# Two-part fp32 matmuls of a streaming trunk: the order of long and short matmuls inside a chunk of weights

## The chip, the core and the metric

The kernel runs on one core of one Trainium2 chip. The metric is device time in microseconds, from the start to the end of an execution; the profile is of one such execution.

## What is computed

A trunk of two layers on 256 tokens of width 2048, in float32. Each layer is a token mixer and a squared-ReLU MLP, both behind an RMSNorm and added to the stream:

```
for layer in range(2):
    hn = rms_norm(h, mix_norm[layer])
    mix = swa_sink_attention(hn, ...) if layer == 0 else rglru_block(hn, ...)
    h = h + mix
    h = h + jnp.square(relu(rms_norm(h, mlp_norm[layer]) @ w_up[layer])) @ w_down[layer]
return rms_norm(h, final_norm)
```

The widths are 2048 to 2560 (query, key, value), 2048 to 2048 (attention's output), 2048 to 8192 to 2048 (each MLP), 2048 to 4096 (into the recurrent block) and 2048 to 2048 (out of it). Nearly all work is in these products.

## The kernel before

Everything is kept transposed: 128 channels on the partitions, the 256 tokens along a row. A product `w.T @ x` takes a 128 x 128 piece of the weights as the stationary operand and the tokens as the moving one.

**Two parts.** Weights and activations are each split into a high part, rounded to the matmul's fp32r type, and a low part, the rest. Of the four partial products three are made. A *long* matmul (L1307) takes the high weights and streams 512 columns, the 256 tokens' high parts and then their low parts, into the two halves of a PSUM bank. A *short* one (L1310) takes the low weights and streams the 256 high parts into the second half of the same bank, where they are added.

**Tiling.** Weights come in chunks of 512 input rows by 256 output columns (512 KB), already laid out so in memory. Four chunks (`CHUNKS`) cover the 2048 input rows and make a pair: two blocks (`b`) of 128 output columns, in two PSUM banks. Two pairs are a quad (512 output columns), and `ps` has a bank for each of its four blocks. In a chunk there are four row blocks (`CH_KT`, index `k`) and two column blocks `b`, so 8 long and 8 short matmuls. `products` issues them: for each `k` long `b`=0, long `b`=1, short `b`=0, short `b`=1. The text calls these four a group. There are 85 quads, 680 chunks.

**Who does what.** SyncE loads chunks into 8 slots (`w_raw`), each as soon as VectorE has made the low half of the slot's chunk before. ScalarE copies a chunk to `w_hi` (L370, `next_hi`), VectorE subtracts for `w_lo` (L812, `next_lo`). `w_hi` and `w_lo` have four slots, one for each chunk of a pair, so a slot is refilled when TensorE has done the same chunk of the pair before: the last short matmul of a chunk raises `wts_used`. Before a chunk TensorE waits for `lo_ready`, for the operand (`xn_ready` or `mid_ready`) and, before the first chunk of a pair, for `psum_free`. At a pair's end ScalarE copies the second halves of the banks out (L383), VectorE adds the first halves (L826), and the pair's own step follows: rope and softmax, the residual sum and the next norm's operand, or the squared ReLU.

**The order of the work** is written out by hand. Each engine runs attention's 5 quads, the output's 4, an MLP of 32, the recurrent mixer's 8 and 4, and the second MLP of 32. An MLP has four turns of four quads up and four quads down. The MLP's norm needs the sum over all channels of the squares: `stats(norm)`, two small fp32 matmuls (L1334 and L1335) that TensorE makes behind the first pair of the MLP; ScalarE then takes the root (L412) and VectorE its inverse (L836). Attention puts scores, transposes and outputs between chunks (`between` of `pair`), the recurrent mixer its gates: `gates` makes 24 matmuls of the short one's shape through `three` (L1327 to L1329), each three adding to the same 256 columns. `late_quad` is the first quad of each output product, whose last chunk has weight tiles of its own, `gate_hi` and `gate_lo`. The execution ends with sums (L1496) and 16 and more 128 x 128 transposes (L1489).

Of the kernel before, what the change touches and what calls it, by code (L numbers as in the profile page):

```python
# [27 lines left out]
PART = 128  # L28
TOK = 256
D = 2048  # L30
KT = D // PART
# [11 lines left out]
CH_KT = 4  # L43
PAIR_N = 256
CHUNKS = KT // CH_KT
WARM_UP = 22
SLOTS = 2 * CHUNKS

# [8 lines left out]
QB_IN = QB_MLP0 + Q_MLP  # L57
# [60 lines left out]
def build(nc, x_l, vec_d, const_d, w_qkv, w_o, w_in, ga_w, gx_w, w_out, w_up, w_down, out_l):  # L118
# [12 lines left out]
    with ctx:  # L131
# [1164 lines left out]
        def _(pe):  # L1296
            def products(q, half_i, s, operand, ready_sem, ready, late=False):

                pe.wait_ge(lo_ready, (q * 2 + half_i) * CHUNKS + s + 1)
                if s == 0 and not (isinstance(q, int) and q == 0):  # L1300
                    pe.wait_ge(psum_free, q * 2 + half_i - 1)
                pe.wait_ge(ready_sem, ready + 2 * s + 2)
                hi, lo = late_w if late else (w_hi[:, s], w_lo[:, s])
                for k in range(CH_KT):
                    kt = s * CH_KT + k
                    for b in range(2):
                        nc.tensor.matmul(ps[:, 2 * half_i + b, :], hi[:, k, b * PART:(b + 1) * PART],  # L1307
                                         operand[:, :, kt, :], start=kt == 0, stop=False)
                    for b in range(2):
                        last = nc.tensor.matmul(ps[:, 2 * half_i + b, TOK:2 * TOK], lo[:, k, b * PART:(b + 1) * PART],  # L1310
                                                operand[:, 0, kt, :], start=False, stop=kt == KT - 1)
                last.then_inc(wts_used, 1)

            def pair(q, half_i, operand, ready_sem, ready, between=None):

                for s in range(CHUNKS):
                    products(q, half_i, s, operand, ready_sem, ready)
                    if between and s in between:
                        between[s]()

            def quad(q, operand, ready_sem, ready, between=None, between_b=None):
                pair(q, 0, operand, ready_sem, ready, between)
                pair(q, 1, operand, ready_sem, ready, between_b)

# [85 lines left out]
            def attention_pair(q, half_i, j, g, g_before):  # L1410

                between = {3: lambda: scores_and_output(j, g, g_before)}
                if g_before is not None:
                    between[2] = lambda: transpose_probs(j - 1)
                pair(q, half_i, *qkv, between)

# [28 lines left out]
            def mlp(base, norm, mid_base):  # L1445
                operand = (xn, xn_ready, 8 * norm)
                quad(base, *operand, {3: lambda: stats(norm)})
                with pe.Fori(1, 4) as i:
                    quad(i + base, *operand)
                with pe.Fori(0, 4) as i:  # L1450
                    quad(i + (base + 4), mid, mid_ready, mid_base)
                with pe.Fori(1, GROUPS) as g:
                    with pe.Fori(0, 4) as i:
                        quad(g * 8 + i + base, *operand)
                    with pe.Fori(0, 4) as i:
                        quad(g * 8 + i + (base + 4), mid, mid_ready, g * PAIRS + mid_base)

# [123 lines left out]
```

## Time and profile before

| | us |
|---|---|
| median of 3 runs | 1996.04 (1995.44 to 1996.25) |
| the profiled execution | 1995.82 |
| its span, first to last instruction | 1993.7 |
| TensorE busy | 1982.3 (99%) |
| weight loads busy | 1736.9 (87%) |
| VectorE busy | 1368.5 (69%) |
| ScalarE busy | 1062.1 (53%) |

The span is the time between the first and the last instruction in the profile, on which all times in its rows are counted. Of an engine's rows the duration runs from the start of an instruction to its end; TensorE's matmuls overlap, so the time that one costs is read from start to start. In a timeline row "x2" are two instructions of one kind in a row, with the time from the first one's start to the last one's end.

### The profile page before, as it was taken

How to read it: one execution, taken by the hardware profiler on the slowest of the kernel's cores; microseconds unless marked ns; L12 is line 12 of the kernel's file. 1: busy time of each engine (PE TensorE's matmuls, PEld its weight loads, DVE VectorE, ACT ScalarE, POOL GpSimd, SP SyncE). 2: the span in 40 equal slices, each digit the busy share in tenths (PEclk: the TensorE clock that was granted, in tenths of full speed). 3: DMA queues.
4: the chain of work that ended last, by engine and by line, in shares of the span. 5: the costliest groups of instructions: out<-in, count | busy, mean ns of one | idle time of the engine just before them, and what ended most of it. 6: DMA issues, size and time to landing. Idle time of an engine off the chain costs nothing.

```text
span 1993.7 us, 34015 instructions
## 1 busy us (share of the span) xinstructions
PE 1982.3 (99%) x11542; PEld 1736.9 (87%) x11542; DVE 1368.5 (69%) x1575; ACT 1062.1 (53%) x1446; POOL 7.4 (0%) x11
## 2 busy tenths in 40 slices
PE   9999999999999999999999999999999999999998
PEld 8898888888888888888888888888888888888887
DVE  8998676556656665666789997766566556656664
ACT  6666554444444444445588885544444444444453
POOL 1000000000000000000000000000000000000000
PEclk9999999999999999999999999999999999999999
DMA  7434555555555555555555545565556555555652
GB/s 287 158 127 158 181 189 191 188 191 188 189 190 180 197 186 191 177 175 199 190 190 189 189 169 192 188 197 184 193 184 187 192 182 197 189 189 178 195 175 95
DMA packets 104187, 368.17 MB, mean 185 GB/s; under 512 B 11472, under 2 KB 15696, under 8 KB 104016
## 3 DMA queue, kind: packets, MB, share of 16 engines
q1 hardware_dynamic: 103856, 365.53, 55.4%
q0 software_dynamic: 288, 2.10, 0.3%
q8 instruction: 24, 0.39, 0.1%
q14 instruction: 19, 0.16, 0.0%
HBM read 365.48 MB, written 2.10 MB: 184 GB/s over the span
## 4 chain that ended last, share of the span: by engine, by line
PE 94%; DVE 3%; ACT 2%; issue 1%; DVEq 0%; ACTq 0%; POOL 0%; POOLq 0%
PE ps L1307 61%; PE ps L1310 30%; DVE w_lo L812 1%; ACT h L467 1%; PE aux L1327 1%; PE aux L1328 1%; PE aux L1329 1%; PE aux L1399 0%; ACT w_hi L370 0%; DVE h L923 0%; DVE h L934 0%; PE aux L1382 0%; DVE u L826 0%; DVE pt L939 0%; DVE u L899 0%
## 5 line engine op out<-in xcount | busy, mean ns | idle before, releaser
L812 DVE TENSOR_TENSOR w_lo<-w_raw,w_hi 128x1024 fp32r<-128x1024 f32 x678 | 815.8, 1222 | 336.2 <-ACT w_hi L370 335.1
L370 ACT ACTIVATE w_hi<-w_raw 128x1024 fp32r<-128x1024 f32 x678 | 701.4, 1054 | 448.3 <-PE ps L1310 445.5
L1307 PE MATMUL ps<-xn,w_hi 128*128 128x512 f32 x2880 | 906.4, 396 | 0.2 <-DVE w_lo L812 0.2
L1307 PE MATMUL ps<-mid,w_hi 128*128 128x512 f32 x2544 | 799.4, 396 | 1.1 <-DVE w_lo L812 0.6
L1310 PEld LDWEIGHTS ps<-xn,w_lo 128*128 128x128 f32 x2880 | 541.0, 188 | 127.9
L1310 PEld LDWEIGHTS ps<-mid,w_lo 128*128 128x128 f32 x2544 | 477.9, 188 | 113.0
L1310 PE MATMUL ps<-xn,w_lo 128*128 128x256 f32 x2880 | 566.1, 278 | 0.0
L1310 PE MATMUL ps<-mid,w_lo 128*128 128x256 f32 x2544 | 499.9, 278 | 0.0
L1307 PEld LDWEIGHTS ps<-xn,w_hi 128*128 128x128 f32 x2880 | 438.9, 189 | 1.2 <-issue 0.5
L1307 PEld LDWEIGHTS ps<-mid,w_hi 128*128 128x128 f32 x2544 | 387.3, 189 | 1.8 <-DVE w_lo L812 1.0
L826 DVE TENSOR_TENSOR u<-ps,half 128x512 f32<-128x512 f32 x169 | 116.6, 690 | 155.3 <-ACT half L383 136.0
L383 ACT ACTIVATE half<-ps 128x512 f32<-128x512 f32 x153 | 91.6, 599 | 228.7 <-PE ps L1310 228.7
L594 ACT ACTIVATE mid<-u 128x512 f32 (+1 forms) x64 | 40.6, 634 | 105.4 <-DVE u L1054 105.4
L1060 DVE TENSOR_TENSOR mid<-v,mid 128x512 f32 (+1 forms) x64 | 44.3, 693 | 23.0 <-ACT mid L594 22.8
L852 DVE TENSOR_TENSOR h<-h,u 128x512 f32 (+1 forms) x70 | 48.5, 693 | 11.6 <-DVE u L826 11.5
L842 DVE SCALAR_TENSOR_TENSOR xn<-h,vec,xn (+1 forms) x48 | 21.1, 482 | 40.3 <-ACT xn L405 40.3
L1057 DVE TENSOR_TENSOR v<-u 128x512 f32<-128x512 f32 x64 | 44.3, 692 | 2.2
L1054 DVE SCALAR_TENSOR_TENSOR u<-u,rstd 128x512 f32<-128x512 f32 x64 | 44.3, 692 | 2.2
L403 ACT ACTIVATE sq<-h 128x512 f32 (+1 forms) x24 | 15.2, 632 | 41.5 <-DVE h L852 40.0
L831 DVE TENSOR_TENSOR acc<-acc,sq 128x512 f32<-128x512 f32 x31 | 21.3, 687 | 5.8 <-ACT sq L772 5.8
L1181 DVE SCALAR_TENSOR_TENSOR xc<-xb,vec,xc 128x256 f32<-128x256 f32 x48 | 21.1, 481 | 4.3 <-ACT xc L686 2.6
L467 ACT ACTIVATE h<-aux,h 128x128 f32<-128x128 f32 x64 | 22.4, 374 | 0.0
(168 smaller groups left out, 762.0 us busy)
## 6 DMA issues: line engine op xcount, KB each, us to landing
w_raw<-mlp_w_up_dram SPq DMA_DIRECT2D x256, 512.0 KB, 4.2
w_raw<-mlp_w_down_dram SPq DMA_DIRECT2D x256, 512.0 KB, 4.2
w_raw<-b_w_in_dram SPq DMA_DIRECT2D x64, 512.0 KB, 4.9
w_raw<-a_w_qkv_dram SPq DMA_DIRECT2D x40, 512.0 KB, 4.8
w_raw<-a_w_o_dram SPq DMA_DIRECT2D x32, 512.0 KB, 4.5
w_raw<-b_w_out_dram SPq DMA_DIRECT2D x32, 512.0 KB, 4.4
h<-x_l_dram SPq DMA_DIRECT2D x4, 512.0 KB, 8.1
gate_raw<-b_gate_a_w_dram SPq DMA_DIRECT2D x8, 256.0 KB, 2.8
```

Source lines behind the costliest of these rows:

```text
L370: nc.scalar.activation(w_hi[:, s, :, :], w_raw[:, slot, :, :], ACT.Copy).then_inc(hi_ready, 1)
L383: nc.scalar.activation(half[:, :, :], src, ACT.Copy).then_inc(half_copied, 1)
L467: last = nc.scalar.activation(out[:, m * PART:(m + 1) * PART], xs[:, b, (m % 4) * PART:(m % 4 + 1) * PART], ACT.Exp, bias=s_neg[:, m:m + 1 ...
L594: nc.scalar.activation(mid[:, 0, bass.ds(j * 2, 2), :], u[:, :, :], ACT.Square).then_inc(mid_hi, 1)
L812: nc.vector.tensor_tensor(w_lo[:, s, :, :], w_raw[:, slot, :, :], w_hi[:, s, :, :].bitcast(F32), ALU.subtract).then_inc(lo_ready, 1)
L826: nc.vector.tensor_tensor(u[:, :, :], ps[:, 2 * half_i:2 * half_i + 2, 0:TOK], half[:, :, :], ALU.add).then_inc(psum_free, 1)
L852: add = nc.vector.tensor_tensor(h_pair(j), h_pair(j), u[:, :, :], ALU.add)
L1054: nc.vector.scalar_tensor_tensor(u[:, :, :], in0=u[:, :, :], scalar=0.0, in1=bc2(rstd[:, :]), op0=ALU.max, op1=ALU.mult).then_inc(relu_rea ...
L1057: nc.vector.tensor_tensor(v[:, :, :], u[:, :, :], u[:, :, :], ALU.mult).then_inc(squared, 1)
L1060: nc.vector.tensor_tensor(mid[:, 1, bass.ds(j * 2, 2), :], v[:, :, :], mid[:, 0, bass.ds(j * 2, 2), :].bitcast(F32), ALU.subtract).then_in ...
L1307: nc.tensor.matmul(ps[:, 2 * half_i + b, :], hi[:, k, b * PART:(b + 1) * PART], operand[:, :, kt, :], start=kt == 0, stop=False)
L1310: last = nc.tensor.matmul(ps[:, 2 * half_i + b, TOK:2 * TOK], lo[:, k, b * PART:(b + 1) * PART], operand[:, 0, kt, :], start=False, stop=k ...
```

## The change

The matmuls of a chunk are now issued by two small functions, `long` and `short`, and `products` has two orders. The old one stays for the first and late quads, for attention's output and the mixers' first pairs. The new one (`in_turn`) takes for each `b` the four `k`, and for each a long and then its short matmul. It is used for the first three chunks of six attention pairs, for the recurrent mixer's quads from the second on, and for all quads of both MLPs but the first one; there the first pair keeps the old order. The second pair of that quad, behind `stats`, is issued by a new function `apart`: 24 long matmuls of three chunks, then their 24 short ones, then the fourth chunk in turn. Each chunk's waits stand ahead of its long matmuls, and `wts_used` rises behind its short ones.

```diff
+RUN = 3
...
-            def products(q, half_i, s, operand, ready_sem, ready, late=False):
+            def chunk_ready(q, half_i, s, ready_sem, ready):
                 pe.wait_ge(lo_ready, (q * 2 + half_i) * CHUNKS + s + 1)
                 if s == 0 and not (isinstance(q, int) and q == 0):
                     pe.wait_ge(psum_free, q * 2 + half_i - 1)
                 pe.wait_ge(ready_sem, ready + 2 * s + 2)
+            def long(half_i, hi, s, k, b, operand):
+                kt = s * CH_KT + k
+                nc.tensor.matmul(ps[:, 2 * half_i + b, :], hi[:, k, b * PART:(b + 1) * PART],
+                                 operand[:, :, kt, :], start=kt == 0, stop=False)
+            def short(half_i, lo, s, k, b, operand):
+                kt = s * CH_KT + k
+                return nc.tensor.matmul(ps[:, 2 * half_i + b, TOK:2 * TOK], lo[:, k, b * PART:(b + 1) * PART],
+                                        operand[:, 0, kt, :], start=False, stop=kt == KT - 1)
+            def products(q, half_i, s, operand, ready_sem, ready, late=False, in_turn=False):
+                chunk_ready(q, half_i, s, ready_sem, ready)
                 hi, lo = late_w if late else (w_hi[:, s], w_lo[:, s])
...
+                if in_turn:
                     for b in range(2):
+                        for k in range(CH_KT):
+                            long(half_i, hi, s, k, b, operand)
+                            last = short(half_i, lo, s, k, b, operand)
+                else:
+                    for k in range(CH_KT):
+                        long(half_i, hi, s, k, 0, operand)
+                        long(half_i, hi, s, k, 1, operand)
+                        short(half_i, lo, s, k, 0, operand)
+                        last = short(half_i, lo, s, k, 1, operand)
                 last.then_inc(wts_used, 1)
...
+            def apart(q, half_i, operand, ready_sem, ready):
+                for s in range(RUN):
+                    chunk_ready(q, half_i, s, ready_sem, ready)
+                    for k in range(CH_KT):
+                        for b in range(2):
+                            long(half_i, w_hi[:, s], s, k, b, operand)
+                for s in range(RUN):
+                    for k in range(CH_KT):
+                        for b in range(2):
+                            last = short(half_i, w_lo[:, s], s, k, b, operand)
+                    last.then_inc(wts_used, 1)
+                for s in range(RUN, CHUNKS):
+                    products(q, half_i, s, operand, ready_sem, ready, in_turn=True)
...
-                pair(q, half_i, *qkv, between)
+                pair(q, half_i, *qkv, between, (0, 1, 2) if g_before is not None else ())
...
+            whole = tuple(range(CHUNKS))
...
-                quad(base, *operand, {3: lambda: stats(norm)})
+                pair(base, 0, *operand, {3: lambda: stats(norm)})
+                apart(base, 1, *operand)
                 with pe.Fori(1, 4) as i:
-                    quad(i + base, *operand)
+                    quad(i + base, *operand, None, whole)
                 with pe.Fori(0, 4) as i:
-                    quad(i + (base + 4), mid, mid_ready, mid_base)
+                    quad(i + (base + 4), mid, mid_ready, mid_base, None, whole)
...
-                quad(n + QB_IN, *lru_in, {0: lambda: gates(n - 1)})
+                quad(n + QB_IN, *lru_in, {0: lambda: gates(n - 1)}, whole)
```

How the instructions move on TensorE is seen at two places. The first is a chunk in the loop over an MLP's second to fourth quads, before:

```order
L1299 REGISTER_ALU
L1307 MATMUL ps<-xn,w_hi 128x512 [waits xn_ready,lo_ready]
L1307 MATMUL ps<-xn,w_hi 128x512
L1310 MATMUL ps<-xn,w_lo 128x256 x2
L1307 MATMUL ps<-xn,w_hi 128x512 x2
L1310 MATMUL ps<-xn,w_lo 128x256 x2
```

and now, its first half (the long matmul is L1308 and the short one L1314 there):

```order
L1300 REGISTER_ALU
L1308 MATMUL ps<-xn,w_hi 128x512 [waits xn_ready,lo_ready]
L1314 MATMUL ps<-xn,w_lo 128x256
L1308 MATMUL ps<-xn,w_hi 128x512
L1314 MATMUL ps<-xn,w_lo 128x256
L1308 MATMUL ps<-xn,w_hi 128x512
L1314 MATMUL ps<-xn,w_lo 128x256
```

The two long ones of a group stood side by side, and the two short ones; now every short one stands between two long ones. The waits are the same, ahead of the chunk's first matmul.

The second place is TensorE behind the sum of squares of the first MLP (`aux<-acc,ones` are the two matmuls of `stats`), before:

```order
L1334 MATMUL aux<-acc,ones 128x256 [waits acc_ready]
L1335 MATMUL aux<-acc,ones 128x256
L1307 MATMUL ps<-xn,w_hi 128x512 [waits xn_ready,psum_free,lo_ready]
L1307 MATMUL ps<-xn,w_hi 128x512
L1310 MATMUL ps<-xn,w_lo 128x256 x2
L1307 MATMUL ps<-xn,w_hi 128x512 x2
```

and now:

```order
L1369 MATMUL aux<-acc,ones 128x256 [waits acc_ready]
L1370 MATMUL aux<-acc,ones 128x256
L1308 MATMUL ps<-xn,w_hi 128x512 [waits xn_ready,psum_free,lo_ready]
L1308 MATMUL ps<-xn,w_hi 128x512 x7
L1308 MATMUL ps<-xn,w_hi 128x512 [waits xn_ready,lo_ready]
L1308 MATMUL ps<-xn,w_hi 128x512 x7
L1308 MATMUL ps<-xn,w_hi 128x512 [waits xn_ready,lo_ready]
L1308 MATMUL ps<-xn,w_hi 128x512 x7
L1314 MATMUL ps<-xn,w_lo 128x256 x24
L1308 MATMUL ps<-xn,w_hi 128x512 [waits xn_ready,lo_ready]
L1314 MATMUL ps<-xn,w_lo 128x256
L1308 MATMUL ps<-xn,w_hi 128x512
```

The long matmuls of three chunks have moved ahead of all their short ones, and with them the waits of the second and third chunk; the fourth chunk's wait stands where it stood.

## Rows read from the trace of the kernel before

**Rows 1.** The page: the span, each engine's busy time, the granted clock in 40 slices.

```profile
span 1993.7 us, 34015 instructions
PE 1982.3 (99%) x11542; PEld 1736.9 (87%) x11542; DVE 1368.5 (69%) x1575; ACT 1062.1 (53%) x1446; POOL 7.4 (0%) x11
PEclk9999999999999999999999999999999999999999
```

**Rows 2.** Waits of TensorE, longest and shortest of seven: us in total, times, longest us.

```profile
PE aux L1399 <- POOL eps L345: 1.1, 1, 1.1
...
PE aux L1382 <- DVE mid L946: 0.3, 1, 0.3
```

**Rows 3.** The page's costliest groups: the long matmuls (xcount, busy us, mean ns).

```profile
L1307 PE MATMUL ps<-xn,w_hi 128*128 128x512 f32 x2880 | 906.4, 396 | 0.2 <-DVE w_lo L812 0.2
L1307 PE MATMUL ps<-mid,w_hi 128*128 128x512 f32 x2544 | 799.4, 396 | 1.1 <-DVE w_lo L812 0.6
```

**Rows 4.** Windows, tile w_hi, MLPs: length, busy us (count) of PE, PEld, DVE, ACT; clock.

```profile
300.00:900.00 600.00, 540.91 (x1724) 262.29 (x1724) 259.52 (x215) 222.58 (x214) 1.00 0.58 188
1300.00:1900.00 600.00, 540.97 (x1723) 262.29 (x1724) 261.38 (x216) 223.90 (x215) 1.00 0.58 188
```

**Rows 5.** Timeline of TensorE, first MLP: start us, time us, engine, line, operation.

```profile
602.23 0.40 PE L1310 MATMUL ps<-mid,w_lo 128*128 128x256 f32 x2
602.47 0.63 PE L1307 MATMUL ps<-mid,w_hi 128*128 128x512 f32 x2
602.94 0.39 PE L1310 MATMUL ps<-mid,w_lo 128*128 128x256 f32 x2
603.16 0.63 PE L1307 MATMUL ps<-mid,w_hi 128*128 128x512 f32 x2
```

**Rows 6.** Timeline of the weight loads, same place.

```profile
600.61 0.42 PEld L1310 LDWEIGHTS ps<-mid,w_lo 128*128 128x128 f32 x2
600.96 0.31 PEld L1307 LDWEIGHTS ps<-mid,w_hi 128*128 128x128 f32 x2
```

**Rows 7.** Timeline of TensorE, the last gates: first and last of 24.

```profile
1173.16 0.29 PE L1327 MATMUL aux<-xc_split,gate_hi 128*128 128x256 f32 x1
...
1175.91 0.28 PE L1329 MATMUL aux<-xc_split,gate_lo 128*128 128x256 f32 x1
```

**Rows 8.** Timeline, the tail's transposes and the row behind them on TensorE.

```profile
1982.14 1.94 PE L1489 MATMUL aux<-const,h 128*128 128x128 f32 x16
...
1983.92 0.96 PE L1496 MATMUL ps<-ones,sq 128*128 128x8 f32 x8
```

**Rows 9.** Timeline of TensorE, the late chunk of attention's output.

```profile
189.86 0.62 PE L1307 MATMUL ps<-mid,gate_hi 128*128 128x512 f32 x2
190.32 0.40 PE L1310 MATMUL ps<-mid,gate_lo 128*128 128x256 f32 x2
...
191.95 0.62 PE L1307 MATMUL ps<-mid,gate_hi 128*128 128x512 f32 x2
192.40 0.40 PE L1310 MATMUL ps<-mid,gate_lo 128*128 128x256 f32 x2
192.63 0.40 PE L1307 MATMUL ps<-mid,w_hi 128*128 128x512 f32 x1
```

**Rows 10.** Timelines of TensorE, ScalarE and VectorE behind the first MLP's sum of squares.

```profile
271.35 0.81 PE L1307 MATMUL ps<-xn,w_hi 128*128 128x512 f32 x2
...
279.91 0.62 PE L1307 MATMUL ps<-xn,w_hi 128*128 128x512 f32 x2
...
282.70 0.63 PE L1307 MATMUL ps<-xn,w_hi 128*128 128x512 f32 x2
...
276.68 2.94 ACT L370 ACTIVATE w_hi<-w_raw 128x1024 fp32r<-128x1024 f32 x3
...
277.76 4.73 DVE L812 TENSOR_TENSOR w_lo<-w_raw,w_hi 128x1024 fp32r<-128x1024 f32 x4 [0.19 <-ACT w_hi L370]
```

**Rows 11.** Windows, first MLP: length, busy us (count) of PE, PEld, DVE, ACT, POOL; clock.

```profile
400.00:600.00 200.00, 200.00 (x1150) 174.51 (x1149) 122.13 (x124) 89.22 (x98) 0.00 (x0) 1.00 0.58 188
```

More of the change, by code:

```diff
@@ L1303, in products @@
+            def products(q, half_i, s, operand, ready_sem, ready, late=False, in_turn=False):
+                chunk_ready(q, half_i, s, ready_sem, ready)
                 hi, lo = late_w if late else (w_hi[:, s], w_lo[:, s])
-                for k in range(CH_KT):
-                    kt = s * CH_KT + k
+                if in_turn:
                     for b in range(2):
[L1307 to L1311, printed above, removed]
@@ L1312, in products @@
-                last.then_inc(wts_used, 1)
-            def pair(q, half_i, operand, ready_sem, ready, between=None):
+                        for k in range(CH_KT):
[7 more added lines that the diff above has]
+                        last = short(half_i, lo, s, k, 1, operand)
@@ L1316, in pair, with quad @@
+            def pair(q, half_i, operand, ready_sem, ready, between=None, in_turn=()):
                 for s in range(CHUNKS):
-                    products(q, half_i, s, operand, ready_sem, ready)
+                    products(q, half_i, s, operand, ready_sem, ready, in_turn=s in in_turn)
                     if between and s in between:
                         between[s]()
-            def quad(q, operand, ready_sem, ready, between=None, between_b=None):
-                pair(q, 0, operand, ready_sem, ready, between)
-                pair(q, 1, operand, ready_sem, ready, between_b)
+            def quad(q, operand, ready_sem, ready, between=None, in_turn=()):
+                pair(q, 0, operand, ready_sem, ready, between, in_turn)
+                pair(q, 1, operand, ready_sem, ready, None, in_turn)
@@ L1446, in mlp @@
                 operand = (xn, xn_ready, 8 * norm)
-                quad(base, *operand, {3: lambda: stats(norm)})
+                pair(base, 0, *operand, {3: lambda: stats(norm)})
+                apart(base, 1, *operand)
                 with pe.Fori(1, 4) as i:
-                    quad(i + base, *operand)
+                    quad(i + base, *operand, None, whole)
                 with pe.Fori(0, 4) as i:
-                    quad(i + (base + 4), mid, mid_ready, mid_base)
+                    quad(i + (base + 4), mid, mid_ready, mid_base, None, whole)
                 with pe.Fori(1, GROUPS) as g:
                     with pe.Fori(0, 4) as i:
-                        quad(g * 8 + i + base, *operand)
+                        quad(g * 8 + i + base, *operand, None, whole)
                     with pe.Fori(0, 4) as i:
-                        quad(g * 8 + i + (base + 4), mid, mid_ready, g * PAIRS + mid_base)
+                        quad(g * 8 + i + (base + 4), mid, mid_ready, g * PAIRS + mid_base, None, whole)
             mlp(QB_MLP0, 1, MID_MLP0)
```

## The prediction

> **What bounds the kernel now.** I read the page first. TensorE is busy for 99% of the span, its weight loads for 87%, VectorE for 69%, ScalarE for 53%, and the granted clock stands at 1.00, the upper of its two levels (2.4 GHz) [rows 1]. A busy TensorE can hide waits, so next come its waits: seven in the view, from 1.1 us down to 0.3 us in total each, so under 8 us in the whole execution [rows 2]. Nothing that VectorE, ScalarE or the queues do is worth more than that. What counts is how fast TensorE gets through its own list.
>
> That list is nearly all one pattern. The page counts 2880 + 2544 = 5424 long matmuls of 512 columns [rows 3]; the code issues 680 chunks of 8 long and 8 short, 5440 of each. In two stretches of 600 us inside the MLPs 1724 and 1723 long matmuls were done, so a group of two long and two short takes 600 / 862 = 0.696 us [rows 4]. The timeline splits it: the two short ones take 0.24 and 0.22 us, 0.23 in the mean, from the first one's start to the next long one's, 115 ns each, and the rest is 0.696 - 0.230 = 0.466 us, 233 ns for each long one [rows 5]. The repetition is even, whatever VectorE and ScalarE do beside it. At a column for each cycle of 2.4 GHz 512 columns would be 213 ns and 256 columns 107 ns, so a group has 56 ns over its bare columns. The weight loads tell where this may sit: each starts with the matmul before its own (the loads for two short ones begin at 600.61, those for two long ones at 600.96, 0.35 us later, which is a long and a short step) and shows some 190 ns, longer than a short matmul's whole step of 115: two of them overlap in 0.31 us [rows 6]. So loads overlap one another, and every matmul has exactly one load beside it. The question of this change is whether a matmul's step depends on its neighbours.
>
> **The change, part by part.**
>
> 1. *Long and short in turn.* No matmul, load, wait or semaphore is added or taken away; 16 matmuls of a chunk change places between the same waits. It concerns 249 chunks in each of the two MLPs (256 less the first 4, less 3 that go apart), 7 x 8 = 56 in the recurrent mixer and 6 x 3 = 18 in attention: 572 chunks, 2288 groups. Each nanosecond of a group is worth 2.3 us.
>
> What a short matmul costs alone between long ones no row of before shows. The nearest rows give a direction. Where short matmuls of the same shape stand 24 in a row (the gates), the 23 steps from 1173.16 to 1175.91 us take 119.6 ns each [rows 7]. Two in a row take 115 each. Sixteen 128-column transposes, each with a load of the same size and a shorter stream, take (1983.92 - 1982.14) / 16 = 111 ns [rows 8]; I read that as about what a load needs. A short matmul is hardly longer than its load, so in a row of them a load that comes late makes the next one late, while a long matmul leaves over 100 ns to catch up. By that reading a single short one goes on from 119.6 and 115 to about 111. The long step I leave at 233, since nothing says that its neighbours change. A group is then 2 x (233 + 111) = 688 ns, 8.1 less: 2288 x 8.1 = **18.5 us less**.
>
> Bounds from both sides. Below: with another weight tile (gate_hi, gate_lo in the late chunk) the same order of matmuls takes 2.77 / 4 = 0.6925 us for a group, its long ones 227.5 ns and its short ones 119 [rows 9], so a step does move by some nanoseconds with how loads and streams meet. The lowest of each, 227.5 and 111, make 677 ns: 19.1 x 2288 = 44 us less. Above: the short one at 119.6, long unchanged, 705 ns: 9.1 x 2288 = 21 us more.
>
> The Trainium skill (TensorE: Matmul & The Clock Gate, section Step-by-step: what each phase is for) says that the array has separate read ports for the moving operand and the weights, so that loading the next weights does not slow the running matmul. By that rule the order of equal work is free and this part is 0 us, not 18.5 us less; the trace does not bear the rule out fully, as the late chunk's change of weight tile alone moves the steps [rows 9].
>
> 2. *24 long, then 24 short.* Two places, 48 shorts in all, which I put at the gates' 119.6: 48 x 4.6 ns = 0.2 us more; if long ones in a row differ by 5 ns either way, it is 48 x 5 = 0.2 us. What it moves is the release of weights. In the pair behind the first MLP's sum of squares (it begins at 271.35 us) ScalarE may refill the slot of the first chunk only after 24 long and 8 short, at 271.5 + 24 x 0.233 + 8 x 0.120 = 278.1 us. Today ScalarE, held up by the root and the first square, gets to that copy as the second of three from 276.68, so at about 277.7; it would be 0.4 us later. The two copies behind it may then start at 279.1 and 280.0, again within half a microsecond of today. VectorE makes the low half of that first chunk as the second of four from 277.76, ready about 280.1, and TensorE needs it with the next pair at 282.70 [rows 10]: 2.6 us of cover, 2.2 afterwards. The last chunk of the same pair is the tight one: its low half is ready at about 279.0 (first of the four), TensorE comes to it at 279.91 today and at about the same time apart, since only the order of the first three chunks changes. Cost nothing; without that cover it would be under 1 us, twice. No queue is passed, as the loads from memory wait for the low halves and not for TensorE.
>
> 3. *Attention and recurrent mixer.* Included in the 2288. In attention other engines often set the pace, so its 72 groups (0.6 us) may give nothing. VectorE at 61% and ScalarE at 45% in the MLP stretch [rows 11] keep room for a TensorE that is 1 or even 5% faster.
>
> Sum: -18.5 + 0.2 = -18.3 us. The profiled execution took 1995.82 us (span 1993.7 and 2.1 around it), 0.2 below the median of 1996.04. On the median: **1977.7 us**.
>
> **The rivals.**
>
> - *Nothing changes, 1996 us.* Each matmul keeps one load beside it and long and short ones their steps. For it: the evenness of the pattern, and that a sum by neighbour is zero if a step depends on its own kind alone. Against: 119.6, 115 and 119 ns for the same shape in different company [rows 5, 7, 9]. A measurement of this kernel can tell about 0.2%, 4 us; that is 1.8 ns in a group of 696, so exact neutrality is a narrow target.
> - *Slower, 2017 us.* In turn, the four long and four short matmuls of each 128 output columns of a chunk write one PSUM bank in a row, and each short one adds to the columns that the long one before it has just written. Today the bank changes with every matmul. The gates' matmuls, three adding to the same columns of one bank, are the slow ones at 119.6 [rows 7], so what I took for crowded loads can be the price of the same bank. If it applies to the short ones, 9.1 ns a group, 21 us; if the long ones rise by 3 ns too, 15 ns and 35 us, 2031 us. It decides as soon as this price is over what the spacing of loads gives back, about 4 ns for a short matmul. Against it no row speaks, since none has a long and a short one in turn; only its size is open, as the same 119.6 can come from crowded loads.
> - *Much faster, 1868 us.* Were the steps to fall to their columns at the granted 1.00, a group is 640 ns and the gain 2288 x 56 = 128 us. Against it: no row of the main pattern comes near it. The Trainium skill (the same page, section Back-to-back issue gap) gives N / 2.4 + 2.5 ns for a warm matmul, 650 ns a group and an estimate of 105 us less; today's trace with 696 is above that rule.
> - *It does less than it says, about 1987 us.* The even pattern may be a rhythm into which loads and streams fall after each interruption, and a new order may find the good rhythm in one MLP only: half of the gain.
>
> **How the numbers follow.** Forecast 0.50, less than it says 0.08, much faster 0.05, unchanged 0.14, slower by the bank 0.23. Faster by over 0.2% is 0.50 + 0.08 + 0.05, less 0.01 for the part of these cases that lies inside 4 us, 0.62; within 0.2% is 0.14 + 0.01 = 0.15; slower is 0.23. The forecast alone reaches from 1952 (44 us less) to 1990. The range goes up into the slower rival, 2014, and down to 1940, past the lowest sum of rows because long steps in new company are unknown; what is left out is the far end of the slower case and most of the much faster one, 2 in 10 at most.
>
> **What would show it.** In the profile after, count the long matmuls of a 600 us stretch of an MLP: 1744 where the forecast holds (688 ns), 1724 if nothing changes, 1702 for the slower rival (705 ns), 1875 for the much faster one. The start of a short one to the next long one should be 0.11 us, not 0.12. The 24 short ones behind the sum of squares should step by about 120 ns, and a step well below that would speak against the crowding of loads. TensorE's waits should stay under 8 us; a new wait on w_lo at about 280 us would show part 2 wrong. The prediction is wrong if the group count moves by a few per cent or not at all, or if the long step changes: that I took as fixed from no row but today's.

## The result: 2015 us, 0.95% slower

| | before | after |
|---|---|---|
| median of the runs | 1996.12 us | 2014.99 us |
| ratio | | 1.0095, 95% interval 1.0082 to 1.0107 |
| the profiled execution | 1995.82 us | 2014.99 us |
| its span | 1993.7 us | 2013.0 us |

The forecast was 1977.7 us, in a range of 1940 to 2014. The kernel became 19 us slower.

The page of the changed kernel, the rows that answer to [rows 1] and [rows 3]:

```profile
span 2013.0 us, 34015 instructions
PE 2001.0 (99%) x11542; PEld 1747.1 (87%) x11542; DVE 1368.7 (68%) x1575; ACT 1062.4 (53%) x1446; POOL 7.4 (0%) x11
PEclk9999999999999999999999999999999999999999
...
L1308 PE MATMUL ps<-xn,w_hi 128*128 128x512 f32 x2880 | 999.0, 397 | 0.6 <-DVE xn L881 0.4
L1308 PE MATMUL ps<-mid,w_hi 128*128 128x512 f32 x2544 | 880.2, 398 | 1.2 <-DVE w_lo L813 0.7
```

The counts of instructions and the busy times of VectorE and ScalarE are those of before, and so is the clock. TensorE alone is busy for 18.7 us longer. The waits of TensorE, the three longest of nine:

```profile
PE aux L1434 <- POOL eps L346: 1.1, 1, 1.1
PE ps L1308 <- DVE w_lo L813: 0.9, 3, 0.4
PE aux L1362 <- DVE qz L914: 0.9, 1, 0.9
```

No new wait is worth naming: the 19 us lie in the matmuls' own steps. The windows of w_hi (columns as in [rows 4]) show where:

```profile
300.00:900.00 600.00, 600.00 (x1699) 319.09 (x1699) 256.37 (x212) 220.87 (x212) 1.00 0.57 185
1300.00:1900.00 600.00, 600.00 (x1700) 319.11 (x1699) 257.01 (x212) 221.03 (x212) 1.00 0.57 187
```

1699 and 1700 long matmuls in 600 us, where before had 1724 and 1723. A pair of a long and a short one takes 600 / 1699.5 = 353.1 ns instead of 348.1, so 10 ns more for the two pairs that made a group of before. The MLPs have 498 chunks in turn, 1992 groups: 19.9 us. That is the whole loss, and a little more. TensorE's timeline in the first MLP (start us, time us, engine, line, operation):

```profile
400.11 0.40 PE L1308 MATMUL ps<-mid,w_hi 128*128 128x512 f32 x1
400.36 0.28 PE L1314 MATMUL ps<-mid,w_lo 128*128 128x256 f32 x1
400.48 0.40 PE L1308 MATMUL ps<-mid,w_hi 128*128 128x512 f32 x1
400.71 0.28 PE L1314 MATMUL ps<-mid,w_lo 128*128 128x256 f32 x1
400.82 0.40 PE L1308 MATMUL ps<-mid,w_hi 128*128 128x512 f32 x1
401.06 0.28 PE L1314 MATMUL ps<-mid,w_lo 128*128 128x256 f32 x1
401.17 0.40 PE L1308 MATMUL ps<-mid,w_hi 128*128 128x512 f32 x1
...
401.54 0.40 PE L1308 MATMUL ps<-mid,w_hi 128*128 128x512 f32 x1
```

From long to long it is 0.37, 0.34, 0.35 us, then again 0.37: a beat of three pairs, 1.06 us. A chunk has eight pairs and a block four, so the beat belongs to no loop and no tile. From start to start the long ones take 0.25, 0.23 and 0.24 us and the short ones 0.12, 0.11 and 0.11; the forecast had 233 ns for every long one. Now the same order in the same execution, in the recurrent mixer:

```profile
1075.93 0.39 PE L1308 MATMUL ps<-xn,w_hi 128*128 128x512 f32 x1
1076.16 0.28 PE L1314 MATMUL ps<-xn,w_lo 128*128 128x256 f32 x1
1076.28 0.39 PE L1308 MATMUL ps<-xn,w_hi 128*128 128x512 f32 x1
1076.51 0.28 PE L1314 MATMUL ps<-xn,w_lo 128*128 128x256 f32 x1
1076.63 0.39 PE L1308 MATMUL ps<-xn,w_hi 128*128 128x512 f32 x1
...
1077.32 0.39 PE L1308 MATMUL ps<-xn,w_hi 128*128 128x512 f32 x1
```

Here four pairs take 1077.32 - 1075.93 = 1.39 us, 347 ns each, even steps (0.23 us for a long one, 0.12 for a short one) and less than the 348 of before. So the order in turn has two rhythms, and both MLPs ran in the slow one. Behind the sum of squares, the 24 and 24 and what follows:

```profile
271.45 5.82 PE L1308 MATMUL ps<-xn,w_hi 128*128 128x512 f32 x24
277.11 3.04 PE L1314 MATMUL ps<-xn,w_lo 128*128 128x256 f32 x24
279.98 0.40 PE L1308 MATMUL ps<-xn,w_hi 128*128 128x512 f32 x1
...
280.33 0.40 PE L1308 MATMUL ps<-xn,w_hi 128*128 128x512 f32 x1
...
280.69 0.40 PE L1308 MATMUL ps<-xn,w_hi 128*128 128x512 f32 x1
```

The 24 short ones take (279.98 - 277.11) / 24 = 119.6 ns each, as the gates' did. At 279.98 the pairs in turn begin.

### The profile page after: what moved, and what is told of

Its sections match the earlier page's. It is cut to its first block, busy times and chain, and to the rows that moved or that the text cites. A ratio compares the mean times of both kernels' runs of the same rounds, so it can differ in the third digit from the quotient of the medians.

```text
span 2013.0 us, 34015 instructions
## 1 busy us (share of the span) xinstructions
PE 2001.0 (99%) x11542; PEld 1747.1 (87%) x11542; DVE 1368.7 (68%) x1575; ACT 1062.4 (53%) x1446; POOL 7.4 (0%) x11
## 4 chain that ended last, share of the span: by engine, by line
PE 94%; DVE 3%; ACT 2%; issue 1%; DMA 0%; DVEq 0%; SPq 0%; ACTq 0%
PE ps L1308 61%; PE ps L1314 31%; DVE w_lo L813 1%; ACT h L468 1%; PE aux L1362 1%; PE aux L1363 1%; PE aux L1364 1%; ACT w_hi L371 0%; DVE h L924 0%; DMA h<-x_l_dram 0%; DVE h L935 0%; PE aux L1417 0%; DVE u L827 0%; DVE pt L940 0%; DVE u L900 0%
## 5 line engine op out<-in xcount | busy, mean ns | idle before, releaser
L1308 PE MATMUL ps<-xn,w_hi 128*128 128x512 f32 x2880 | 999.0, 397 | 0.6 <-DVE xn L881 0.4
L1308 PE MATMUL ps<-mid,w_hi 128*128 128x512 f32 x2544 | 880.2, 398 | 1.2 <-DVE w_lo L813 0.7
L1314 PE MATMUL ps<-xn,w_lo 128*128 128x256 f32 x2880 | 775.4, 280 | 0.0
L1314 PE MATMUL ps<-mid,w_lo 128*128 128x256 f32 x2544 | 672.7, 280 | 0.0
L1308 PEld LDWEIGHTS ps<-xn,w_hi 128*128 128x128 f32 x2880 | 530.1, 188 | 118.1 <-issue 1.0
L1314 PEld LDWEIGHTS ps<-xn,w_lo 128*128 128x128 f32 x2880 | 540.7, 189 | 13.7
L1308 PEld LDWEIGHTS ps<-mid,w_hi 128*128 128x128 f32 x2544 | 460.3, 188 | 98.1 <-DVE w_lo L813 1.1
L1314 PEld LDWEIGHTS ps<-mid,w_lo 128*128 128x128 f32 x2544 | 480.0, 189 | 22.0
```

Source lines behind the costliest of these rows:

```text
L1314: return nc.tensor.matmul(ps[:, 2 * half_i + b, TOK:2 * TOK], lo[:, k, b * PART:(b + 1) * PART], operand[:, 0, kt, :], start=False, stop=k ...
```

## The experiments

**Is it the PSUM bank?** That was the rival with nearly this result. In the first run the bank changes after every short matmul, in the second each short one writes the other bank than the long one before it.

```diff
-                    for b in range(2):
-                        for k in range(CH_KT):
+                    for k in range(CH_KT):
+                        for b in range(2):
                             long(half_i, hi, s, k, b, operand)
                             last = short(half_i, lo, s, k, b, operand)
```

> The changed kernel with the block b inside of k: long and short are still in turn, but the PSUM bank now changes after every short matmul. Bank theory (writing one bank eight times in a row costs the extra 8 ns of a group): the group falls from 705 back towards 697 ns, 1996 to 2006 us. Run-length theory (every change between long and short costs, whatever the banks): 705 ns stays, 2014 to 2016 us.

```diff
+                    blocks = [(k, b) for k in range(CH_KT) for b in range(2)]
+                    long(half_i, hi, s, *blocks[0], operand)
+                    for n in range(1, len(blocks)):
+                        long(half_i, hi, s, *blocks[n], operand)
+                        short(half_i, lo, s, *blocks[n - 1], operand)
+                    last = short(half_i, lo, s, *blocks[-1], operand)
```

> The changed kernel with each short matmul issued one long matmul later, so that it writes the other bank than the long one just before it; the long one behind it writes the short one's bank. Seven of eight pairs of a chunk are still in turn. Bank theory: if the price lies on a short one that follows a long one into its bank, a pair falls from 353 to about 348 ns and the time to 1996 to 2000 us. Run-length theory: 353 ns a pair within a chunk, 2012 to 2016 us.

2015.11 us (ratio 1.0096, 1.0080 to 1.0111) and 2014.47 us (1.0091, 1.0076 to 1.0107). In the window of 300 to 900 us the first of them has

```profile
300.00:900.00 600.00, 600.00 (x1699) 319.05 (x1698) 256.18 (x212) 220.90 (x213) 1.00 0.57 186
```

the same 1699. The second has 1703: one pair in eight is not in turn there. So the bank does not make this cost, neither on the step from long to short nor on the other. The kernel with 16 groups below bears this out: its order writes one bank eight times in a row, as the changed kernel's does, and it runs at 346.5 ns a pair.

**Are short ones in a row what costs?** This is the forecast's own theory. A chunk becomes 8 long and 8 short matmuls (in the kernel before):

```diff
-                for k in range(CH_KT):
-                    kt = s * CH_KT + k
-                    for b in range(2):
-                        nc.tensor.matmul(ps[:, 2 * half_i + b, :], hi[:, k, b * PART:(b + 1) * PART],
-                                         operand[:, :, kt, :], start=kt == 0, stop=False)
-                    for b in range(2):
-                        last = nc.tensor.matmul(ps[:, 2 * half_i + b, TOK:2 * TOK], lo[:, k, b * PART:(b + 1) * PART],
-                                                operand[:, 0, kt, :], start=False, stop=kt == KT - 1)
+                for k0 in range(0, CH_KT, 4):
+                    for k in range(k0, k0 + 4):
+                        kt = s * CH_KT + k
+                        for b in range(2):
+                            nc.tensor.matmul(ps[:, 2 * half_i + b, :], hi[:, k, b * PART:(b + 1) * PART],
+                                             operand[:, :, kt, :], start=kt == 0, stop=False)
+                    for k in range(k0, k0 + 4):
+                        kt = s * CH_KT + k
+                        for b in range(2):
+                            last = nc.tensor.matmul(ps[:, 2 * half_i + b, TOK:2 * TOK], lo[:, k, b * PART:(b + 1) * PART],
+                                                    operand[:, 0, kt, :], start=False, stop=kt == KT - 1)
```

> The kernel before with every chunk as 8 long and then 8 short matmuls. Run-length theory: long ones near the 227 ns and short ones near the 120 ns that the 24 in a row show, two changes in a chunk instead of eight: 2776 to 2782 ns for a chunk against 2787, so 1989 to 1993 us. Crowding theory of the prediction (short ones in a row cost, long ones do not change): 8 x 233 + 8 x 120 = 2824 ns for a chunk, 2021 us.

2000.17 us, ratio 1.0020 (1.0011 to 1.0029), so between the two expectations and in neither. Its timeline:

```profile
400.85 2.00 PE L1308 MATMUL ps<-mid,w_hi 128*128 128x512 f32 x8
402.69 1.12 PE L1313 MATMUL ps<-mid,w_lo 128*128 128x256 f32 x8
403.64 2.00 PE L1308 MATMUL ps<-mid,w_hi 128*128 128x512 f32 x8
```

Eight short ones take 0.95 us, 119 each, as the theory says. Eight long ones take 1.84 us, 230 each and not 233: here the forecast's "nothing says that its neighbours change" fails. What a short one loses in a row, long ones give back. But my second theory, that each change between long and short has one price, falls as well: two changes in a chunk instead of eight do not pay. Runs of four (2 in place of 4 in the three loops over `k0` and `k`) say it louder:

> The kernel before with four long and then four short matmuls, two such runs in a chunk. If what counts is the number of changes between long and short, this lies between runs of two (697 ns for two long and two short) and runs of eight: 697 to 699 ns, 1996 to 2002 us. If the steps follow the place in the run as the runs of eight show them (long 233, 236, 228, 233; short 114, 119, 120, 120), 1403 ns for eight: 702 ns, 2010 us.

2008.25 us, ratio 1.0061 (1.0046 to 1.0077), near the second of its expectations. In order of the length of a run: 1 gives 2015 (or less, see below), 2 gives 1996, 4 gives 2008, 8 gives 2000. That is no law of the number of changes.

**Is it the width or the weight tile?** In turn, high and low weight tiles alternate as well as widths. With the short matmul as wide as the long one only the tiles do (the low weights then also meet the low activations, a fourth product):

```diff
-                return nc.tensor.matmul(ps[:, 2 * half_i + b, TOK:2 * TOK], lo[:, k, b * PART:(b + 1) * PART],
-                                        operand[:, 0, kt, :], start=False, stop=kt == KT - 1)
+                return nc.tensor.matmul(ps[:, 2 * half_i + b, :], lo[:, k, b * PART:(b + 1) * PART],
+                                        operand[:, :, kt, :], start=False, stop=kt == KT - 1)
```

> The changed kernel with the short matmul made as wide as the long one (512 columns, the low weights times both halves, which adds the fourth product): only the width stops alternating, high and low weight tiles still do. If the change of width makes the cost, every step is 227 ns and a former pair 454 ns. If the alternation of the two weight tiles makes it, steps of 233 to 241 ns stay and a former pair is 466 ns or more. About 11 us per 100 pairs more than now in any case, some 2600 us.

> All matmuls 512 columns wide as in the run before of that kind, but in the old order of two and two (the low weights' product takes both halves, which adds the fourth product). If order counts only through widths that differ, this takes the same as in turn: 226.7 ns for each matmul, 2561 us within 2 us. If the order of the weight tiles counts, it differs by over 5 us.

2561.54 us in turn and 2561.53 us in the old order, one run each. The window of the one in turn:

```profile
300.00:900.00 600.00, 505.02 (x1323) 247.86 (x1321) 199.17 (x165) 170.88 (x164) 1.00 0.44 145
```

1323 matmuls with the high weights and as many with the low ones: 600 / 2646 = 226.8 ns for each. With one width for all, the order is free, to a hundredth of a microsecond, though loads of both tiles alternate as before. This agrees with the Trainium skill's separate read ports for weights and moving operand (TensorE: Matmul & The Clock Gate, Step-by-step: what each phase is for), by which a load takes no read bandwidth from the running matmul. The Trainium skill's formula for the gap of a warm matmul, N / 2.4 + 2.5 (same page, Back-to-back issue gap), gives an estimate of 216 ns; the measured 226.8 is 11 above it.

**Is a short one held by its load?** Two more widths, in turn. 384 columns (192 of each half; for the last 64 tokens the low weights' product is missing):

```diff
+                out = ps[:, 2 * half_i + b, :].rearrange("p (x t) -> p x t", x=2)[:, :, 0:192]
+                return nc.tensor.matmul(out, lo[:, k, b * PART:(b + 1) * PART],
+                                        operand[:, :, kt, 0:192], start=False, stop=kt == KT - 1)
```

> The changed kernel with its short matmuls 384 columns wide (192 of each half), so wider than any load needs; the low weights' product is left out for the last 64 tokens of each 256. Load theory (a short stream of 256 columns ends no earlier than the load beside it, about 120 ns, and the long one behind it pays): nothing is short any more, the steps go to their own width, 227 and about 171 to 173 ns, so 398 to 400 ns a pair. Theory that any change of width costs: 405 ns a pair or more, with long steps of 233 to 241 as now.

> Short matmuls 384 columns wide (low weights' product left out for the last 64 tokens of each 256), in the old order. In turn a pair took 413 ns, 13 over the 400 of runs of one width. If two and two halves the changes and so the cost: 406 to 407 ns a pair, about 2318 us (6.6 ns x 4576 pairs less than 2342 = 2312). If the cost of a pair does not depend on the order at this width: 2340 us.

The times are 2342.10 us in turn and 2341.71 us in the old order, one run each. The 24 short ones in a row, in the one in turn, behind the first MLP's sum of squares:

```profile
312.04 4.35 PE L1315 MATMUL ps<-xn,w_lo 128*128 128x384 f32 x24
316.23 0.39 PE L1308 MATMUL ps<-xn,w_hi 128*128 128x512 f32 x1
```

and its window:

```profile
300.00:900.00 600.00, 572.31 (x1451) 271.04 (x1450) 220.72 (x183) 189.07 (x182) 1.00 0.49 160
```

In a row they step by 4.19 / 24 = 174.6 ns. With the long one's 226.8 a pair would be 401; it takes 600 / 1451 = 413.5. A load that fits beside a step of 119.6 ns is not in the way of one of 174.6, and a pair of two widths still costs 12 ns more than its two parts. So the load theory falls for this cost. And two and two do not halve it: the second expectation of the last run holds, 2340 us.

128 columns (the low weights' product missing for half of the tokens):

```diff
+                return nc.tensor.matmul(ps[:, 2 * half_i + b, TOK:TOK + PART], lo[:, k, b * PART:(b + 1) * PART],
+                                        operand[:, 0, kt, 0:PART], start=False, stop=kt == KT - 1)
```

> The changed kernel with its short matmuls only 128 columns wide (the low weights' product for tokens 128 to 255 left out). Load theory: the step of a short one is set by the load beside it and stays between 105 and 120 ns, and a pair at about 345 to 353 ns. If the stream sets it, the step falls to about 60 ns and a pair below 300 ns.

1957.46 us, one run. The timelines, its 24 in a row and a place in turn:

```profile
275.70 2.79 PE L1314 MATMUL ps<-xn,w_lo 128*128 128x128 f32 x24
...
275.76 2.73 PE L1314 MATMUL ps<-xn,w_lo 128*128 128x128 f32 x23
278.33 0.45 PE L1308 MATMUL ps<-xn,w_hi 128*128 128x512 f32 x1
...
400.08 0.44 PE L1308 MATMUL ps<-mid,w_hi 128*128 128x512 f32 x1
400.36 0.22 PE L1314 MATMUL ps<-mid,w_lo 128*128 128x128 f32 x1
400.42 0.44 PE L1308 MATMUL ps<-mid,w_hi 128*128 128x512 f32 x1
```

The row of 23 is the same stretch without its first matmul. In a row the first one takes 0.06 us and the other 23 (278.33 - 275.76) / 23 = 112 ns each, though the stream is half as long as that of the 120 ns. I read this as the load's own time, as the 111 of [rows 8] had let me guess. In turn the short step is 0.06 us and the long one 0.28 us. By the load theory the step was to stay over 105 ns and the pair at 345 to 353; neither did. But the pair of 340 ns is far from the 300 of the other theory, and only 1 more than 227 + 112. The time of a step can be booked on the neighbour; only the sum of a pair may be read.

**Which part of the change counts?** First the 24 in a row alone, all else in the old order (`if in_turn:` becomes `if False:`); then the turn in the mixers alone (six pairs of attention and the recurrent mixer's input quads from the second on; its output keeps the old order, as in the changed kernel), with both MLPs as before.

> Only the two places of 24 long and 24 short matmuls are kept, everything else in the old order. By the trace of the changed kernel the 48 take what they took before within 0.02 us and no wait is new: 1996.1 us, the same as before within 0.1%. Rival: the later release of the weights costs a wait that the changed kernel's longer list hides, up to 1 us at each place.

> Long and short in turn in the mixers alone (18 chunks of attention, 56 of the recurrent mixer), both MLPs in the old order without the 24 in a row. If each chunk in turn costs 33 ns wherever it stands: 74 chunks, 2.4 us, 1998.4 us. If attention hides its part: 1.9 us, 1997.9 us. If the mixers had a gain of their own: below 1996.

1995.90 us beside 1995.93 (1.0000, 0.9991 to 1.0009): the 24 in a row are free, as forecast. And 1995.24 us beside 1996.01 (0.9997, 0.9987 to 1.0006): no loss of 2.4 us, if anything a gain as the mixers' rhythm of 347 ns suggests (280 or so groups x 3 ns = 0.8 us, an estimate), though the interval does not show it. All of the loss is in the MLPs.

**Longer runs still**: 16 long and 16 short (two chunks of a pair) in the MLPs and the recurrent mixer's later quads; the 24 and 24 stay.

```diff
+                if in_turn == whole:
+                    for first in (0, 2):
+                        for s in (first, first + 1):
+                            chunk_ready(q, half_i, s, ready_sem, ready)
+                            for k in range(CH_KT):
+                                for b in range(2):
+                                    long(half_i, w_hi[:, s], s, k, b, operand)
+                        for s in (first, first + 1):
+                            for k in range(CH_KT):
+                                for b in range(2):
+                                    last = short(half_i, w_lo[:, s], s, k, b, operand)
+                            last.then_inc(wts_used, 1)
+                            if between and s in between:
+                                between[s]()
+                    return
```

> Sixteen long and then sixteen short matmuls (two chunks) in the MLPs and the recurrent mixer's quads from the second on, 554 chunks; the rest in the old order. Fixed costs as measured (13.3 ns over its columns for each matmul, and 17 to 20 ns for each turn from a long run of short ones to long ones): 5564 to 5567 ns for two chunks against 5573, so 277 x 6 to 9 = 1.7 to 2.5 us less, 1993.5 to 1994.3 us, if no wait comes. Rival: the first chunk's weights are released later and the fourth's are needed earlier, and waits on the low halves eat it: 1996 us or more.

1998.76 us, ratio 1.0014 (1.0005 to 1.0023). The rival was right. The longest wait of this kernel, and two runs of 16 long ones from its timeline in the second MLP, which stand 99 times two chunks apart:

```profile
PE ps L1310 <- DVE w_lo L813: 2.7, 5, 1.3
```

```profile
1333.16 3.82 PE L1310 MATMUL ps<-xn,w_hi 128*128 128x512 f32 x16
...
1884.26 3.82 PE L1310 MATMUL ps<-xn,w_hi 128*128 128x512 f32 x16
```

Two chunks take 551.10 / 99 = 5.567 us. In the trace of the kernel before, 790 groups take 550.36 us (1329.95 to 1880.31), so eight of them, two chunks, 5.573 us. The gain forecast for the steps is there, 6 ns for two chunks and under 2 us in all. It is lost elsewhere: waits for low halves have risen from 0.8 us in the kernel before to 2.7, and in the last quads of the first MLP some runs of 16 long ones take 4.0 us (936.13 to 940.14) in place of 3.65, without a wait that the view lists.

**What chooses the rhythm?** Same order, same widths, 353 ns in the MLPs and 347 in the mixer. The old order has a beat too, of two groups: its group lengths in the trace alternate between 698 and 696 ns (second short step 112 or 119, read from start to start). In the changed kernel the turn begins behind 24 short ones in the MLPs, and in the recurrent mixer behind the old order, where the last group (up to 1006.99 us) is of the first kind, with 112; it is fast from there, and again behind each quad's gates. Counted from the sum of squares in the trace of before, the 16th group of the MLP's second pair is of the first kind, the 15th of the second. So I let the turn begin in the MLPs behind 16 groups of the old order, and behind 15. The first:

```diff
                 pair(base, 0, *operand, {3: lambda: stats(norm)})
-                apart(base, 1, *operand)
+                pair(base, 1, *operand)
```

> The changed kernel without the 24 in a row: the pair behind each MLP's sum of squares keeps the old order, 16 groups, and long and short go in turn from the next quad on. The old order alternates between groups of 698 ns (second short step 112) and 695 ns (119); behind 16 groups the last one is of the first kind. Theory of two rhythms, set by where the turn begins: entered there the turn falls into the rhythm of 346.7 ns a pair seen in the recurrent mixer, and keeps it through both MLPs: 3.3 ns less for each of about 2280 groups, 7.5 us, 1988.5 us. Theory that the turn costs in the MLPs for a reason of their own (operands, loops): 353.3 ns a pair and 2015 us.

The second is the same but for the last group of that pair:

```diff
...
                         long(half_i, hi, s, k, 0, operand)
-                        long(half_i, hi, s, k, 1, operand)
-                        short(half_i, lo, s, k, 0, operand)
+                        if last_in_turn and k == CH_KT - 1:
+                            short(half_i, lo, s, k, 0, operand)
+                            long(half_i, hi, s, k, 1, operand)
+                        else:
+                            long(half_i, hi, s, k, 1, operand)
+                            short(half_i, lo, s, k, 0, operand)
                         last = short(half_i, lo, s, k, 1, operand)
...
-                apart(base, 1, *operand)
+                for s in range(CHUNKS):
+                    products(base, 1, s, *operand, last_in_turn=s == CHUNKS - 1)
```

> The same, but the last group of that pair already goes in turn, so the turn begins behind 15 groups of the old order, the last one of the second kind (119). Theory of two rhythms: it falls into the slow one, 353.3 ns a pair, 2014 to 2015 us, 26 us above the kernel that differs from it by the order of four matmuls in two places. Theory that only the 24 in a row brought the slow rhythm: 1988.5 us.

In the third, the turn begins at once behind the two matmuls of the sum of squares (`apart(base, 1, *operand)` becomes `pair(base, 1, *operand, None, whole)`):

> Long and short in turn at once behind the two matmuls of the sum of squares. The first long step there is 418 ns, then the steps are unsettled. Two rhythms: either 1988 us or 2015 us for an MLP that keeps its rhythm, nothing between unless the two MLPs differ (2002 us). Theory of the MLPs' own reason: 2015 us.

| | turn begins | us | ratio, 95% interval |
|---|---|---|---|
| first | behind 16 groups | 1988.65 | 0.9962, 0.9949 to 0.9976 |
| second | behind 15 groups | 2015.37 | 1.0097, 1.0081 to 1.0112 |
| third | at once | 2015.59 | 1.0097, 1.0081 to 1.0112 |

The first two differ by the order of two matmuls at two places of the program, and by 26.7 us. The windows of w_hi, first the one behind 16 groups,

```profile
300.00:900.00 600.00, 600.00 (x1731) 324.48 (x1732) 259.91 (x216) 224.86 (x216) 1.00 0.58 189
1300.00:1900.00 600.00, 600.00 (x1732) 324.56 (x1731) 261.84 (x216) 225.19 (x216) 1.00 0.58 189
```

and the one behind 15:

```profile
300.00:900.00 600.00, 600.00 (x1699) 319.06 (x1698) 256.60 (x212) 220.97 (x212) 1.00 0.57 185
1300.00:1900.00 600.00, 600.00 (x1700) 319.11 (x1699) 257.10 (x212) 221.27 (x212) 1.00 0.57 187
```

600 / 1731.5 = 346.5 ns for a pair, which is 226.8 + 119.6, the sum of a long and a short one each among its like. The rhythm that is caught at the start lasts, through loops and quads, for hundreds of microseconds. The timelines at the entry, fast,

```profile
282.95 0.40 PE L1308 MATMUL ps<-xn,w_hi 128*128 128x512 f32 x1
283.18 0.28 PE L1314 MATMUL ps<-xn,w_lo 128*128 128x256 f32 x1
283.30 0.39 PE L1308 MATMUL ps<-xn,w_hi 128*128 128x512 f32 x1
...
283.64 0.40 PE L1308 MATMUL ps<-xn,w_hi 128*128 128x512 f32 x1
```

and slow:

```profile
282.08 0.40 PE L1308 MATMUL ps<-xn,w_hi 128*128 128x512 f32 x1
282.31 0.28 PE L1314 MATMUL ps<-xn,w_lo 128*128 128x256 f32 x1
282.43 0.40 PE L1308 MATMUL ps<-xn,w_hi 128*128 128x512 f32 x1
...
282.79 0.40 PE L1308 MATMUL ps<-xn,w_hi 128*128 128x512 f32 x1
```

The first pair takes 0.35 us in both. It is the second one that tells: 0.34 us here, 0.36 there.

The entry of the recurrent mixer bears this out in passing. With the turn in the mixers alone, and in the kernel with 16 groups, the last old group there is of the second kind (119), and both run in the slow rhythm from 997.0 and 993.9 us until the first gates, 2.8 us later; behind the gates they are fast. The third kernel, with the turn at once, enters there behind the second kind too, at 1007.1 us, and is slow up to its gates. The second, with 15 groups, enters behind the first kind (112), at 1007.0 us, and is fast.

The kernel with the turn behind 16 groups is faster than both: 7.4 us below before, 26.3 us below the changed one.

## Why the prediction was wrong

- *What bounds the kernel*: right. TensorE's own list, no waits, 56 ns of a group over its bare columns. The runs split these 56: each matmul takes 13 ns over its columns at 2.4 GHz when its neighbours have its width (226.8 against 213, 119.6 against 107), four of them 53, and the old order's beat the 3 that are left.
- *Part 1, the step that failed*: "By that reading a single short one goes on from 119.6 and 115 to about 111", together with "The long step I leave at 233". Both are wrong in kind. Of 119.6 for many short ones and 115 for two I drew a line to one, and held the long one fixed, while a row beside them already said that a pair is to be taken as a whole: in the late chunk [rows 9] the short ones are slow (119) and the long ones fast (227.5), and a pair is 346 ns. The runs of 8 show the same (119 and 230). The sum for a pair in turn was 344; the slow rhythm gives 353.1, with long steps of 0.23 to 0.25 us, the fast one 346.5, with short steps of 0.12, and that is no less than its parts, 226.8 + 119.6. There was no crowding to be relieved: a load takes 112 ns at most (the row of 128-column ones), less than the 119.6 of a short one, and 119.6 is the same 13 ns over its columns that a long one has.
- *The bounds*: the upper one, 21 us, is near the measured 19, but by chance. It put the price on short ones at 119.6 with the long one unchanged. The lower one, 44 us, was reached by no run with these widths: 346.5 ns a pair, 7.4 us below the kernel before, is the lowest.
- *The rival by the bank*, 2017 us: right in size and sign, wrong in cause. Two runs with other banks took 2015.1 and 2014.5 us, and the fast rhythm came with the changed kernel's own order of banks.
- *The rival by rhythm*, "a new order may find the good rhythm in one MLP only": the right mechanism with the wrong signs. It had half of a gain where the bad rhythm is a loss of 19.9 us, and it was given 0.08. The two MLPs did not differ either; the good rhythm was in the mixer.
- *Nothing changes*: holds where all widths are equal (2561.54 and 2561.53 us); not here.
- *Part 2, 24 and 24*: right. The run with it alone took 1995.90 us. The first chunk's copy was to be allowed at 278.1; ScalarE's row has it at

```profile
278.32 2.98 ACT L371 ACTIVATE w_hi<-w_raw 128x1024 fp32r<-128x1024 f32 x3 [0.49 <-PE ps L1314]
```

and the next pair did not wait. What I did not cost is what stands behind it: the 24 short ones leave TensorE where the turn falls into the slow rhythm. In place of this function, the old order for 16 groups brings the fast one.
- *Part 3*: the mixers gave no loss and at most 0.8 us.
- *The chances*: 0.23 stood for slower, all on one mechanism. The point that exact neutrality is a narrow target was sound. The same argument, that a step moves by nanoseconds with its neighbours, gave no reason to prefer one sign so clearly.

Still open is what the rhythm is. The runs show on what it depends (widths that differ, and the entry) and that the order of banks does not make it; with equal widths the order of the weight tiles costs nothing. No run varied what VectorE, ScalarE or the queues do. No row shows the part of TensorE in which the rhythm arises, nor why 384 columns cost 12 ns a pair in both orders. That the kind of the last old group decides is borne out by the four entries into the MLPs of the last two kernels and by the mixer's entry in six (fast in the changed kernel, in the first run on the bank and with 15 groups; slow with the turn in the mixers alone, with 16 groups and with the turn at once); why it does is not shown, nor why 24 short ones lead to the slow rhythm and the gates' 24 to the fast one.

## What to carry to other kernels

When TensorE works without waits, compare whole periods (from one start to the same place many periods on, or time over count in a long window), not single steps, since a step's time can be booked on its neighbour. If matmuls of two widths alternate, look for a beat in their starts and at different stages of the same execution: the same order can run in two rhythms, 2% apart here, and what stands just before the stretch chooses. Then vary the entry by one group and measure it before an order is accepted or thrown away, and check the window counts again after every later edit ahead of that place.

## What the runs showed that was not expected

- One order of matmuls, two lasting rhythms: 353.1 and 346.5 ns for 512 + 256 columns, chosen by 15 or 16 groups ahead of it, repeated within 0.9 us in all runs of a kernel.
- A matmul of this type among its like takes 226.8 ns for 512 columns, 174.6 for 384, 119.6 for 256 and 112 for 128: the columns at 2.4 GHz and 13 to 15 ns, and at 128 columns, by my reading, its load.
- The time by length of the runs of long and short ones is not monotonic: 4 and 4 cost 12 us more than 2 and 2, 8 and 8 only 4 us more; 16 and 16 are 6 ns shorter for two chunks where nothing waits, and still 2.8 us longer in all.
